# Feed-forward blocks multiplied in pairs: all rounded rows first, then all remainder rows

## What is computed

```python
def swiglu(x, w_gate, w_up, w_down):
    return (jax.nn.silu(x @ w_gate) * (x @ w_up)) @ w_down

h = h + 0.5 * swiglu(rms_norm(h, norm), gate, up, down)   # 1024 -> 2816 -> 1024
```

## Time and profile before

| | |
|---|---|
| median of three runs | 1050.06 us |
| the profiled execution's span | 1048.1 us |
| TensorE (PE) busy | 99% |
| weight loads (PEld) busy | 89% |
| VectorE (DVE) busy | 77% |
| ScalarE (ACT) busy | 59% |
| GpSimd (POOL) busy | 5% |
| traffic with HBM | 180 GB/s over the span |

### The profile page before, as it was taken

How to read it: one execution, slowest core, us unless ns; L and a number is a source line. 1 busy time by engine, 2 the same in 40 slices (tenths; PEclk the granted TensorE clock), 3 DMA queues, 4 the chain that set the end, 5 groups by cost and what they waited for, 6 DMA issues and landing times.

```text
span 1048.1 us, 18314 instructions
## 1 busy us (share of the span) xinstructions
PE 1039.2 (99%) x6542; PEld 931.7 (89%) x6542; DVE 804.6 (77%) x1192; ACT 616.0 (59%) x979; POOL 51.0 (5%) x70
## 2 busy tenths in 40 slices
PE   9999999999999999999999999999999999999997
PEld 8888888999999988888888888888998998888886
DVE  7888777699768888887766888776689678888663
ACT  7655554478878775555435556543456766556441
POOL 0200012100000000000111000011100000000021
PEclk9999999999999999999999999999999999999999
DMA  9966766559545566666865666676555456667671
GB/s 261 225 189 193 210 195 177 161 152 276 137 120 160 167 197 196 187 195 173 221 182 159 191 193 189 188 219 175 150 166 167 121 156 197 191 192 205 178 205 40
DMA packets 363298, 190.12 MB, mean 181 GB/s; under 512 B 6080, under 2 KB 360672, under 8 KB 363248
## 3 DMA queue, kind: packets, MB, share of 16 engines
q1 hardware_dynamic: 362848, 188.79, 63.7%
q0 software_dynamic: 256, 0.59, 0.3%
q10 hardware_dynamic: 144, 0.10, 0.1%
HBM read 187.86 MB, written 1.07 MB: 180 GB/s over the span
## 4 chain that ended last, share of the span: by engine, by line
PE 95%; DVE 2%; ACT 1%; SPq 1%; issue 1%; DMA 0%; DVEq 0%; ACTq 0%
PE psum L259 46%; PE psum L265 24%; PE psum L240 6%; PE psum L244 6%; PE psum L241 6%; PE psum L1809 1%; PE psum L1814 1%; PE psum L1737 1%; DMA raw<-in_ffn_gate 0%; PE psum L1080 0%; SPq L194 0%; PE psum L1097 0%; DVE xn L355 0%; PE psum L1098 0%; DVE arena L1510 0%
## 5 line engine op out<-in xcount | busy, mean ns | idle before, releaser
L229 DVE TENSOR_TENSOR wlo<-raw,whi 128x1024 fp32r<-128x1024 f32 (+1 forms) x322 | 414.9, 1307 | 68.6 <-ACT whi L224 67.4
L224 ACT ACTIVATE whi<-raw 128x1024 fp32r<-128x1024 f32 (+1 forms) x322 | 351.7, 1113 | 22.7 <-PE psum L244 20.0
L259 PE MATMUL psum<-xn,whi 128*128 128x512 f32 x1392 | 350.4, 393 | 0.4 <-DVE xn L355 0.2
L259 PEld LDWEIGHTS psum<-xn,whi 128*128 128x128 f32 x1392 | 250.6, 189 | 46.2 <-DVE xn L355 1.0
L265 PEld LDWEIGHTS psum<-xn,wlo 128*128 128x128 f32 x1392 | 190.2, 190 | 13.7
L265 PE MATMUL psum<-xn,wlo 128*128 128x256 f32 x1392 | 194.6, 282 | 0.0
L259 PE MATMUL psum<-hid,whi 128*128 128x512 f32 x704 | 171.8, 391 | 0.0
L259 PEld LDWEIGHTS psum<-hid,whi 128*128 128x128 f32 x704 | 128.1, 189 | 24.0
L240 PE MATMUL psum<-xn,whi 128*128 128x256 f32 x416 | 104.5, 289 | 0.0
L241 PE MATMUL psum<-xn,whi 128*128 128x256 f32 x416 | 101.9, 283 | 0.0
L265 PEld LDWEIGHTS psum<-hid,wlo 128*128 128x128 f32 x704 | 92.9, 191 | 4.9
(11 more groups left out here) (248 smaller groups left out, 940.2 us busy)
## 6 DMA issues: line engine op xcount, KB each, us to landing
raw<-in_ffn_down SPq DMA_DIRECT2D x64, 704.0 KB, 4.6
raw<-in_ffn_gate SPq DMA_DIRECT2D x87, 512.0 KB, 3.8
raw<-in_ffn_up SPq DMA_DIRECT2D x87, 512.0 KB, 3.9
raw<-in_hyb_w_in SPq DMA_DIRECT2D x36, 512.0 KB, 4.8
raw<-in_dif_w_qkv SPq DMA_DIRECT2D x24, 512.0 KB, 4.3
raw<-in_hyb_w_out SPq DMA_DIRECT2D x16, 512.0 KB, 4.2
raw<-in_dif_w_o SPq DMA_DIRECT2D x8, 512.0 KB, 3.7
hid<-cs_rows SPq DMA_DIRECT2D x4, 512.0 KB, 7.1
```

Source lines behind the costliest of these rows:

```text
L224: act.activation(whi[:, s, 0:k * P], raw[:, s, 0:k * P], ACT.Copy).then_inc(s_whi, 1)
L229: dve.tensor_tensor(wlo[:, s, 0:k * P], raw[:, s, 0:k * P], whi[:, s, 0:k * P].bitcast(F32), ALU.subtract).then_inc(s_wlo, 1)
L259: mm = pe.matmul(acc, hi[:, j, :], x[:, t, :, :], start=start and j == 0, stop=own and stop and j == k - 1)
```

## The change

In the feed-forward, a pair is multiplied by a new function, `multiply_rows`: the wide matmuls of the first block, the wide ones of the second, the narrow ones of the first, the narrow ones of the second. The number, shapes, operands and banks of the matmuls stay as they are. `s_whi` of the second block is waited for behind the wide matmuls of the first; `s_wlo` of each block before its narrow ones; `s_dhi` is signalled behind the last wide matmul, and each block's `s_blk` behind its last narrow one. The first two pairs of the first feed-forward and the first pair of the others keep the old order.

```diff
+        def multiply_rows(pe, b, k, x, steps, need=None, rounded_done=None):
+
+            for m, (s, k0, acc, rest, opens, closes) in enumerate(steps):
+                pe.wait_ge(s_whi, b + m + 1)
+                for j in range(k):
+                    if need:
+                        need(k0 + j)
+                    mm = pe.matmul(acc, tile_of(whi, s, k)[:, j, :], x[:, k0 + j, :, :], start=opens and j == 0,
+                                   stop=closes and rest is not None and j == k - 1)
             if rounded_done is not None:
                 mm.then_inc(rounded_done, 1)
+            for m, (s, k0, acc, rest, opens, closes) in enumerate(steps):
+                pe.wait_ge(s_wlo, b + m + 1)
+                for j in range(k):
+                    mm = pe.matmul(acc[:, T:2 * T] if rest is None else rest, tile_of(wlo, s, k)[:, j, :], x[:, k0 + j, 0, :],
+                                   start=opens and rest is not None and j == 0, stop=closes and j == k - 1)
                 mm.then_inc(s_blk, 1)
...
-            def gate_up(p, g, need=None, before_up=lambda: None):
+            def gate_up(p, g):
+                multiply_rows(pe, p * 2, DT, xn, [(2 * g + m, 0, wide(g, m), None, True, True) for m in range(2)])
...
             def down(p, g, need=None):
-
-                for m in range(2):
-                    multiply_wide(pe, p * 2 + m, 2 * g + m, KD, hid, m * KD, wide(0, g), start=m == 0, stop=m == 1,
-                                  need=need, rounded_done=s_dhi if m else None, rest=rest_of(g))
+                multiply_rows(pe, p * 2, KD, hid, [(2 * g + m, m * KD, wide(0, g), rest_of(g), m == 0, m == 1) for m in range(2)],
+                              need=need, rounded_done=s_dhi)
...
             if n:
                 read_out(pe, p0 - 2)
-                gate_up(p0, 0, lambda t: pe.wait_ge(s_xlo, DT * n + t + 1), lambda: read_out(pe, p0 - 1))
+                first_gate_up(p0, lambda t: pe.wait_ge(s_xlo, DT * n + t + 1), lambda: read_out(pe, p0 - 1))
                 token_sums(pe, n)
                 gate_up(p0 + 1, 1)
             else:
                 first_pair()
                 zero_products(5)
-                gate_up(p0 + 1, 1, before_up=lambda: token_sums(pe, n))
+                for m in range(2):
+                    if m:
+                        token_sums(pe, n)
+                    multiply_wide(pe, 2 * (p0 + 1) + m, 2 + m, DT, xn, 0, wide(1, m))
```

More of the change, by code:

```diff
@@ L246, in multiply, with multiply_wide @@
                 mm.then_inc(s_blk, 1)
-        def multiply_wide(pe, b, s, k, x, k0, acc, start=True, stop=True, need=None, part=None, rounded_done=None,
-                          rest=None):
+        def multiply_wide(pe, b, s, k, x, k0, acc, need=None, part=None):
             hi, lo = tile_of(whi, s, k), tile_of(wlo, s, k)
             pe.wait_ge(s_whi, b + 1)
-            own = rest is not None
-            rest = rest if own else acc[:, T:2 * T]
             for j in part or range(k):
-                t = k0 + j
@@ L257, in multiply_wide @@
                 if need:
-                    need(t)
-                mm = pe.matmul(acc, hi[:, j, :], x[:, t, :, :], start=start and j == 0,
-                               stop=own and stop and j == k - 1)
+                    need(k0 + j)
+                pe.matmul(acc, hi[:, j, :], x[:, k0 + j, :, :], start=j == 0, stop=False)
+            pe.wait_ge(s_wlo, b + 1)
+            for j in part or range(k):
+                mm = pe.matmul(acc[:, T:2 * T], lo[:, j, :], x[:, k0 + j, 0, :], start=False, stop=j == k - 1)
@@ new lines, in multiply_wide @@
+            if j == k - 1:
+                mm.then_inc(s_blk, 1)
+        def multiply_rows(pe, b, k, x, steps, need=None, rounded_done=None):
[3 more added lines that the diff above has]
+                    if need:
+                        need(k0 + j)
+                    mm = pe.matmul(acc, tile_of(whi, s, k)[:, j, :], x[:, k0 + j, :, :], start=opens and j == 0,
+                                   stop=closes and rest is not None and j == k - 1)
@@ L535, in ffn_tensor, with first_gate_up @@
             p0, p1, hb = first[n], first[n] + FT, hidden_before(n)
-            def gate_up(p, g, need=None, before_up=lambda: None):
-                for m in range(2):
[L540 to L544, removed]
+            def gate_up(p, g):
+                multiply_rows(pe, p * 2, DT, xn, [(2 * g + m, 0, wide(g, m), None, True, True) for m in range(2)])
+            def first_gate_up(p, need, before_up):
+                for part in early_tiles(n):
+                    multiply_wide(pe, p * 2, 0, DT, xn, 0, wide(0, 0), need=need, part=part)
+                before_up()
+                multiply_wide(pe, p * 2 + 1, 1, DT, xn, 0, wide(0, 1))
             def down(p, g, need=None):
-                for m in range(2):
-                    multiply_wide(pe, p * 2 + m, 2 * g + m, KD, hid, m * KD, wide(0, g), start=m == 0, stop=m == 1,
-                                  need=need, rounded_done=s_dhi if m else None, rest=rest_of(g))
+                multiply_rows(pe, p * 2, KD, hid, [(2 * g + m, m * KD, wide(0, g), rest_of(g), m == 0, m == 1) for m in range(2)],
+                              need=need, rounded_done=s_dhi)
             def zero_products(count):
```

## The result

The changed kernel takes 1052.69 us (median of seven runs, 1052.53 to 1053.32); the kernel before, run beside it, 1049.72 us (1049.31 to 1050.50). The ratio is 1.0027, 95% interval 1.0018 to 1.0037: slower by 3.0 us, with an interval from 1.9 to 3.9 us. The forecast was 1053.0, 2.9 us slower.

The account below looks back on a forecast made before the run. TensorE, busy 99% of the span, was taken as the bound. Four stalls, +4.8 us, and 107 pairs' savings, -1.9 us, gave +2.9 on 1050.06: 1053.0 us, with 1052.2 to 1053.8 at chance 0.65 and a wider range of 1051.4 to 1055.3.

Parts of the forecast that it names:

- Term 1: Gate/up and down pairs: half the wide/narrow switches saves 0.018 us a pair, 2.1 us over 115 pairs if nothing else happens.
- Rival 1: Feed-forward pairs: halving the switches gives nothing and each stall costs 1.25 us, in all +5.0 us: 1055.1; chance 0.12.
- Term 2: First down pair of each phase: TensorE stalls 1.15 us for hidden tile 21, losing 1.21 us a phase, +4.8 us.
- Rival 3: First down pairs: the stall is smaller, 0.4 to 0.9 us a phase, giving 1050.5 to 1052; chance 0.10.
- Rival 2: First down pairs: hidden tile 21 is there in time, ending 1.15 us sooner, only interval savings remain: 1048.0; chance 0.05.
- (a): Gate/up: the second block's rounded weights are wanted 0.95 us earlier, at no cost against a margin of 4.7 us.
- (b): Gate/up: first block released 1.82 us later, making ScalarE's work at most some 0.1 us late, at no cost.
- (e): Down pairs: s_dhi comes 1.3 us earlier, so two adds run earlier, but nothing is gained at the phase ends.
- Rival 4: A second wait, from the first block's late release or the stall: 0.4 to 2 us more, 1053.5 to 1055.5; chance 0.08.

Follow-up runs that it names:

- only_first_down: The kernel before, with the new order only in the first down pair of each feed-forward: 1054.80 us, ratio 1.0046.
- first_down_old: The changed kernel, but the first down pair of each feed-forward keeps the old order: 1047.93 us, ratio 0.9977 to the kernel before.
- tile21_earlier: The changed kernel, with ScalarE's and VectorE's queues reordered so hidden tile 21 is made ahead of block 45's split: 1047.83 us, ratio 0.9979 to the kernel before.
- half_the_gap: The kernel before, only each feed-forward's first down pair reordered: 21 wide matmuls, five narrow, the 22nd wide, the other narrow ones: 1051.91 us, one run.
- gate_up_only: The changed kernel with the new order in gate/up alone, all down pairs in the old order: 1048.55 us, ratio 0.9984 to the kernel before.
- twice_the_switches: The kernel before, with gate/up blocks multiplied as 4 wide, 4 narrow, 4 wide, 4 narrow, down in its old order: 1052.36 us, ratio 1.0021.

## Why the prediction was right

**Term 1, the intervals: right.** Taken as 0.018 us a pair, measured as 0.021 from the periods (5.587 to 5.566 and 7.667 to 7.646), which two-decimal rows give to about 0.003. So it was a little small: 115 x 0.021 is 2.4 us, the upper bound that was given, in place of 2.1. The choice between switch and wait, made from one stretch of attention's matmuls, holds: doubling the switches cost 2.3 us, and moving the waits away left the period as it was. The Trainium skill ("TensorE: Matmul & The Clock Gate", section "Wait — 56ns, not 53.3ns?") gives back-to-back matmuls their columns at 2.4 GHz and a fixed amount, 215.7 ns from start to start at 512 columns. The trace doesn't agree: here it is 227 ns once a run has settled, and up to 236 ns at its start, and the same matmuls in another order took another time. Rival 1 falls.

**Term 2, the last hidden tile: right in place, mechanism and size.** Forecast: a stall of 1.15 us, found 1.15 to 1.16; 1.21 us a phase, found 8.91 - 7.68 = 1.23, less 0.02 that the down start moved, so 1.21. That the tile keeps its distance of 5.87 us from down's start was the step on which all hung. It held in each run that left the two queues alone, with 5.84 to 5.90 us in all phases. only_first_down isolates the term at 4.8 us, first_down_old and tile21_earlier take it away in two independent ways, half_the_gap halves it. Rival 3 falls with them. Its lower end had been worked out too high: by the prediction's own terms a stall of 0.4 us costs 1.21 - 0.75 = 0.46 us a phase, which gives 1050.0 us and not 1050.5. Nothing else hung on that.

The reason for the constant distance had less room than it seemed. In the first feed-forward, the corrections copy of tile 20 had waited 0.46 us for TensorE; in the changed kernel no wait is listed before it:

```profile
125.98 0.42 ACT L630 ACTIVATE hid<-arena 128x256 fp32r<-128x256 f32 x1 [1.05 <-DVE arena L708]
126.44 0.60 ACT L621 ACTIVATE arena<-psum 128x512 f32<-128x512 f32 x1
```

ScalarE's instruction before ended at 125.98 + 0.42 = 126.40, so only 0.04 us were left. TensorE came 0.41 us sooner here (126.24 in place of 126.65), and the tile came sooner by as much. Had TensorE gained more ahead, the tile could not have followed, and the stall would have grown. That is worked out from these rows; no run shows it.

**Rival 2** was priced right and given its point of decision rightly: tile21_earlier brings the tile 1.5 us sooner, over the 1.15 us that were named, and the time goes to 1047.83 us, where 1048.0 had been worked out. It needed an edit that the change doesn't have.

**The moves at no cost: right, as far as shown.** (a), (b): gate_up_only gains the 1.5 us that were forecast. The delay of (b) is there, and of the size given. Late in the second feed-forward, ScalarE's copy of a first block starts 0.42 us behind the start of the hidden-hi step and no longer 0.33, and recurs at TensorE's pace of 5.57 us in place of 5.46:

```profile
461.61 1.04 ACT L224 ACTIVATE whi<-raw 128x1024 fp32r<-128x1024 f32 x1
...
467.07 1.06 ACT L224 ACTIVATE whi<-raw 128x1024 fp32r<-128x1024 f32 x1
...
472.21 0.42 ACT L630 ACTIVATE hid<-arena 128x256 fp32r<-128x256 f32 x1 [1.05 <-DVE arena L708]
472.63 1.06 ACT L224 ACTIVATE whi<-raw 128x1024 fp32r<-128x1024 f32 x1
...
478.20 1.06 ACT L224 ACTIVATE whi<-raw 128x1024 fp32r<-128x1024 f32 x1
```

These 0.09 us are too short to be listed as a wait. What the list shows is the other side: held to TensorE's pace here, the corrections copy waited for TensorE for 2.9 us in 3 places, where it had waited 11.0 us in 17. (e): VectorE's first add (L786, the old L774) now follows the earlier signal, and the third waits longer at the phase's end,

```profile
558.29 0.42 DVE L791 SCALAR_TENSOR_TENSOR h<-psum,h 128x256 f32<-128x256 f32 x1 [1.75 <-PE psum L276]
```

1.75 us in place of the 0.43 of the earlier trace rows. Nothing was gained there, as said. Rival 4, a second wait, doesn't show: besides the 4.0 us TensorE waits in the places of before.

**The sum.** 4 x 1.21 = 4.8 us of loss and 107 x 0.018 = 1.9 us of gain gave +2.9; measured +3.0. The two terms measured separately are +4.8 (only_first_down) and -2.1 (first_down_old, 111 pairs), and 4.8 - 2.1 = 2.7 agrees with the change's 3.0 within the intervals. That 2.9 and 3.0 lie 0.1 us apart is in part luck: with the 0.021 us that the periods give, the sum is 4.8 - 107 x 0.021 = 2.6 us, the spans differ by 2.7, and the interval of the measured 3.0 is 2 us wide.

## What to carry to other kernels

When the work of the busiest engine is regrouped, look first at what each moved instruction waits for: this order took 0.02 us off each of 115 pairs and lost more at four matmuls that moved 1.3 us forward, to 1.15 us ahead of their operand. The numbers to look for are the margin in front of a moved instruction, here 0.26 us, and the length of the queue that makes its operand; the loads of the engines that make it, 59% and 77%, say nothing of either. If the operand is late only because unrelated work stands ahead of it in an in-order queue, reorder that queue: here this turned 3.0 us slower into 2.2 us faster with the same matmuls.

## What the runs showed of the hardware

A run of wide matmuls behind narrow ones starts slower than it goes on. Single starts in the traces of the kernel before and the change give, in the mean, 233, 236, 228, 233 and 231 ns for its first five intervals and 226.7 ns from then on, 27 ns over in all, whether the run has 8, 11, 16 or 22 matmuls. The first two narrow ones behind a wide run are shorter (113 and 119 ns, then 120), which gives 7 ns back. The 20 ns that are left are the 0.021 us of the periods. In twice_the_switches the runs of four give 22 ns over and 6 back, 16 in all. It is the same in gate/up, where wide and narrow ones write one bank, and in down, where they write two. Alternating 256-column matmuls of other phases (L240, L241) show 120 ns throughout, and attention's wide ones of two lines 227 to 228. What makes the slow start is open; no run here looks inside it. Also, a matmul that had to wait is followed by its successor after 0.34 us in place of 0.227, so that each such wait cost 0.11 us beyond its own length.
